# The input loaded channel-major in pieces, and one narrow projection placed on the two column halves of TensorE

## The chip, the core and the metric

The kernel runs as one program on one core of a Trainium2 chip. TensorE multiplies matrices into PSUM (8 banks of 128 partitions by 512 floats), VectorE, ScalarE and GpSimd work on SBUF and PSUM, and SyncE (SP) issues most of the transfers from and to the chip's memory. The metric is the device time of one execution in microseconds; the kernel before was executed three times, and its median is 2150.88 us. All data is float32.

## The reference

A block of 1024 tokens with 1024 channels passes two layers of computation. The first layer, to which the change belongs, begins with one wide projection of x:

```
proj = einsum("bsd,de->bse", x, w_in[l])
q, k, v, g_a, x_b, g_b, c_cols, g_c = split(proj, split_idx)
y_a = _swa_sinks(q, k, v, attn_sinks[l])        # attention over a window of 128, 8 query heads, 2 key heads
y_b = _rg_lru(x_b, ...)                         # convolution, gates, linear recurrence
y_c, v_own = _rwkv7(c_cols, rwkv_mu[l], ...)    # c_cols: r, k, v (256 each), decay input (32), rate input (32)
out = einsum("bse,ed->bsd", concat(y_a*silu(g_a), y_b*silu(g_b), y_c*silu(g_c)), w_out[l])
x = layer_norm(ALPHA * x + out)
```

`q` has 512 columns. The decay and rate inputs of the third branch are 64 columns together. Behind this stand a pooling mixer, a mixture of experts, a latent attention, a second mixture of experts and a final norm; the change does not touch their code.

## The kernel before

Every product of the first stage has channels on the contracting side, so the kernel needs x with channels on partitions: `xT`, 8 groups of 128 channels by 1024 tokens. The host hands x over token-major. `sp_first` loads it in 8 row tiles of 128 tokens by 1024 channels into `x_bufs`, with the query weights (`w_in_q`, 2 MB) behind the first four tiles. `pe_first` transposes each tile on TensorE (8 transposes of 128x128 into two PSUM banks), ScalarE copies the one bank and VectorE the other into `xT`. It handles tiles 0 to 3 (the left token half), makes four query projections for these 512 tokens, handles tiles 4 to 7, and makes the other four.

A projection (`proj`, `pe_project`) is 128 columns of weights against 512 tokens: 8 products, one for each group of channels, summed in one PSUM bank. The list `proj` gives the order: q (8), k (2), the gate of the attention (8, up to here `N_EARLY`), and then the ones that fill TensorE during the windowed attention (`pe_swa`). Banks 6 and 7 hold projections (`pj`), banks 0 to 5 the rest (`sw`). Each of the objects `pj` and `sw` hands out its banks in turn, and the user of a bank waits until the engine named in the list has emptied it.

The windowed attention runs over 8 blocks of 128 tokens with a software pipeline four deep (`turns(NT, 4)`). In turn t TensorE does the weighted sum of block t-3 (`pv`), the transposes of the probabilities of block t-2 (`tr`), the projections that `fills_at(t)` names, and the scores of block t (`sc`). Between the scores of a block and its transposes lie VectorE and ScalarE: mask, row maximum, exponential, sum, division; VectorE signals `normed` at the end. The decay/rate input (`wa`, 64 columns) is two entries of `proj`, one for each token half; both stand in turn 4. The weights of a group lie in one of two buffers (`w_view`), and SP reloads a buffer when the last projection from it is done. After turn 10 comes `prep`, which waits for everything of the attention (`after_swa`).

A product is a line

```
return e.matmul(out, lhsT, rhs, start=start, stop=stop, skip_group_check=True)      # line 221
```

so line 221 carries nearly all products of the program, and the shapes tell them apart. One float32 product appears in the trace as two MATMUL records, one transpose as one. "128\*64" in a record means that the weights have 128 rows and 64 columns. Already in the kernel before, the experts' products use the two column halves of the array when a block of 128 rows holds tokens of two experts: `pe_gate_up` and `pe_down` go over `shares(ws)`, which gives rows 0 to 63 with the one expert's weights and rows 64 to 127 with the other's, in turn:

```
for k in range(KD):
    for rows, w in shares(ws):
        m = mm(e, ring.bank[key][rows], xt[:, k, rows], gu_weights(w)[:, k, :], k == 0, k == KD - 1)
```

Of the kernel before, what the change touches and what calls it, by code (L numbers as in the profile page):

```python
# [14 lines left out]
P = 128  # L15
# [4 lines left out]
HD = 64  # L20
# [169 lines left out]
def build(nc, io):  # L190
    ctx = ExitStack()
    with ctx:
# [86 lines left out]
        base_b1 = top[0]  # L279
        x_bufs = [take(D) for _ in range(NT)]  # L280
        d_row = [landed(f"row{i}") for i in range(8)]
        d_win = [landed(f"w_in{i}") for i in range(2)]
        m_x = [d.nth() for d in d_row]
        LOADS = ["q", "kv", "ga", "rk", "vwa", "lru", "gc"]
        m_w = {name: d_win[i % 2].nth() for i, name in enumerate(LOADS)}
        w_view = {name: w_bufs[i % 2].rearrange("p a b -> p (a b)")[:, 0:KD * WIDTH[name]].rearrange("p (a b) -> p a b", a=KD)
# [35 lines left out]

        order = []
        for i in range(NT):
            order += [(("x", i, 0), "S"), (("x", i, 1), "V")]
        order += [(("v", g), "S") for g in range(2)]
# [26 lines left out]

        def x_ready(half):
            return [sw.empty(("x", 4 * half + 3, 0)), sw.empty(("x", 4 * half + 3, 1))]

        def pe_project(e, n):
            group, c0, width, half, kind, _ = proj[n]
            if n == first_of[group]:
                e.wait_ge(*m_w[group])  # L360
            if kind == "q":
                wait_all(e, x_ready(half))
            wait_all(e, pj.free(n))
            out = pj.bank[n][0:width, :]
            for k in range(KD):
                i = mm(e, out, w_view[group][:, k, c0:c0 + width], xT[:, k, half_cols(half)], k == 0, k == KD - 1)
            i.then_inc(*pj.fill(n))

        def act_project(e, n):
            group, c0, width, half, kind, j = proj[n]  # L370
            if kind == "k":
                return
            e.wait_ge(*pj.full(n))
            ps = pj.bank[n][0:width, :]
# [7 lines left out]
            out, scale = {"q": lambda: (qT[:, j, c:c + 512], HD ** -0.5), "rkv": lambda: (rkv[:, j, 1 + c:513 + c], 1.0),  # L382
                          "wa": lambda: (wa[0:64, 1 + c:513 + c], 1.0), "xb": lambda: (xb[:, j, 3 + c:515 + c], 1.0)}[kind]()
            e.activation(out, ps, ACT.Copy, bias=0.0, scale=scale).then_inc(*pj.drain(n, "S"))  # L384

# [14 lines left out]
        def pe_first(e):  # L400
            e.wait_ge(*m_const)
            for half in range(2):
                for i in range(4 * half, 4 * half + 4):
                    e.wait_ge(*m_x[i])
                    for hf in range(2):
                        key = ("x", i, hf)
                        wait_all(e, sw.free(key))
                        for k in range(4):
                            m = e.transpose(four(sw.bank[key])[:, k, :], x_bufs[i][:, P * (4 * hf + k):P * (4 * hf + k + 1)], ident)
                        m.then_inc(*sw.fill(key))  # L410
                for n in range(4 * half, 4 * half + 4):
                    pe_project(e, n)
            for n in range(8, 10):
                pe_project(e, n)
            for g in range(2):
# [7 lines left out]
                m.then_inc(*sw.fill(key))  # L423
            for n in range(10, N_EARLY):
                pe_project(e, n)

        def act_first(e):
            for half in range(2):
                for i in range(4 * half, 4 * half + 4):
                    key = ("x", i, 0)  # L430
                    e.wait_ge(*sw.full(key))
                    e.activation(xT[:, 0:4, P * i:P * (i + 1)], four(sw.bank[key]), ACT.Copy, bias=0.0).then_inc(*sw.drain(key, "S"))
# [3 lines left out]
                for n in range(4 * half, 4 * half + 4):  # L436
                    act_project(e, n)
# [4 lines left out]
            for n in range(10, N_EARLY):  # L442
                act_project(e, n)

        def dve_first(e):
            for i in range(NT):
                key = ("x", i, 1)
                e.wait_ge(*sw.full(key))
                e.tensor_copy(xT[:, 4:8, P * i:P * (i + 1)], four(sw.bank[key])).then_inc(*sw.drain(key, "V"))
                if i == 3:  # L450
                    dve_softplus(e)
            for n in range(8, N_EARLY):
                dve_project(e, n)
# [63 lines left out]
        def pe_swa(e):  # L517
            for d, n in turns(NT, 4):
# [25 lines left out]
                elif d == 0:  # L544
                    for f in fills_at(n):
                        pe_project(e, f)
                    if n == 0:
                        e.wait_ge(*pj.empty(7))
                        e.wait_ge(*pj.empty(9))
                    c0, k0, wd = window_cols(n)  # L550
# [103 lines left out]

        N_SWA = N_EARLY + 2 * NT + 4

        def sp_first(e):
            e.dma_start(chan, io["chan"]).then_inc(d_chan.sem, 16)
            for i in range(NT):
# [4 lines left out]
            e.wait_ge(*pj.full(last_of["q"]))  # L664
            e.dma_start(w_view["ga"], io["w_in_ga"]).then_inc(d_win[0].sem, 16)
# [2524 lines left out]
```

## Time and profile before

| | us |
|---|---|
| median of 3 executions | 2150.88 (2149.66 to 2151.88) |
| span of the profiled execution, first to last instruction | 2143.7 |
| TensorE busy | 2004.4 (94% of the span) |
| VectorE busy | 812.5 |
| ScalarE busy | 532.2 |
| TensorE not yet started | 5.3 |

The profile gives the span of the profiled execution and no total time for it. The three timed executions lie 6.0 to 8.2 us above that span; this is what lies around the first and the last instruction. Busy times are sums over all stages; which engine sets the end in a stage has to be read from its waits.

### The profile page before, as it was taken

The numbers are of one execution on the slowest core, as the hardware profiler recorded it, in microseconds if no ns is written. First come the engines' busy times: TensorE is split into PE (matmuls) and PEld (weight loads), VectorE is DVE, ScalarE is ACT, GpSimd is POOL, SyncE is SP. The second block draws the span as 40 slices with busy tenths as digits, with TensorE's granted clock in tenths as the row PEclk, the third lists the DMA queues.
The fourth block names the chain that finished last, engine by engine and source line by source line (L and its number), as shares of the span: only waits on it lengthen the run. The fifth ranks groups of instructions, "written<-read, shape, count | busy, mean of one in ns | idle before, by whom it ended". The sixth has DMA issues, their size and how long they took to land. (4 is left out here: it accounts for less than half of the span.)

```text
span 2143.7 us, 28374 instructions
## 1 busy us (share of the span) xinstructions
PE 2004.4 (94%) x11085; PEld 1161.1 (54%) x11085; DVE 812.5 (38%) x1889; ACT 532.2 (25%) x1294; POOL 188.4 (9%) x283
## 2 busy tenths in 40 slices
PE   8999999889997988999998999999999988999990
PEld 4545554488543964444445657777675554444440
DVE  1114555867353463111115524444352134111115
ACT  1003233433111321111133433333331110111112
POOL 0000002001162211000002000000000001000003
PEclk9999999989998989999999999999999988999995
DMA  3500100020021147999985000000020018999987
GB/s 138 226 28 6 40 20 4 1 82 4 2 90 53 41 175 302 403 423 426 424 335 204 23 0 1 1 1 1 1 80 23 30 46 331 387 425 424 425 354 265
DMA packets 51389, 334.68 MB, mean 156 GB/s; under 512 B 6832, under 2 KB 7152, under 8 KB 33200
## 3 DMA queue, kind: packets, MB, share of 16 engines
q1 hardware_dynamic: 39376, 289.63, 33.1%
q0 software_dynamic: 11872, 43.13, 5.5%
q8 instruction: 93, 1.52, 0.3%
q14 instruction: 48, 0.39, 0.1%
HBM read 285.48 MB, written 47.25 MB: 155 GB/s over the span
## 5 line engine op out<-in xcount | busy, mean ns | idle before, releaser
L221 PE MATMUL psum<-arena 128*128 128x512 f32 (+12 forms) x9694 | 1863.2, 385 | 79.6 <-issue 29.0
L221 PEld LDWEIGHTS psum<-arena 128*128 128x128 f32 (+3 forms) x9694 | 1010.5, 168 | 877.7 <-issue 783.6
L2193 DVE TENSOR_TENSOR arena<-psum,arena 128x256 f32<-128x256 f32 x50 | 21.2, 425 | 423.1 <-ACT arena L2243 423.1
L1541 ACT ACTIVATE arena<-arena 128x1024 f32<-128x1024 f32 x43 | 45.4, 1056 | 249.7 <-DVE arena L2940 105.6
L2279 POOL DMA_INDIRECT arena<-xn_rows,arena x50 | 47.2, 944 | 657.4 <-PE psum L2154 443.4
L2243 ACT ACTIVATE arena<-psum 128x256 f32<-128x256 f32 x50 | 19.2, 385 | 322.0 <-PE psum L221 322.0
L2853 ACT ACTIVATE arena<-psum,arena 128x1024 f32<-128x1024 f32 (+8 forms) x72 | 50.2, 699 | 188.6 <-DVE arena L2889 188.6
L1242 ACT ACTIVATE arena<-psum 128x256 f32<-128x256 f32 (+3 forms) x128 | 44.0, 356 | 102.3 <-PE psum L221 91.4
L2236 ACT ACTIVATE arena<-psum 128x512 f32<-128x512 f32 x50 | 29.9, 597 | 148.1 <-PE psum L221 148.1
L2882 DVE TENSOR_TENSOR psum<-psum,arena 128x128 f32<-128x128 f32 (+2 forms) x72 | 20.3, 283 | 103.5 <-PE psum L221 103.2
L2387 DVE SCALAR_TENSOR_TENSOR arena<-arena 128x1024 f32<-128x1024 f32 (+1 forms) x34 | 43.5, 1281 | 30.7 <-DMA arena<-expert_rows,arena 29.4
L2266 DVE COPY arena<-psum 128x512 f32<-128x512 f32 x50 | 34.6, 692 | 54.1 <-PE psum L221 54.1
L2154 PE MATMUL psum<-arena 128*128 128x128 f32 x400 | 51.8, 273 | 0.0
L2884 DVE TENSOR_REDUCE arena<-psum 128x1 f32<-128x1024 f32 (+8 forms) x72 | 50.8, 706 | 2.5
L2905 DVE COPY arena<-psum 128x512 f32<-128x512 f32 (+3 forms) x48 | 22.8, 489 | 76.0 <-PE psum L2808 75.9
L2224 ACT ACTIVATE arena<-psum 128x512 f32<-128x512 f32 x50 | 29.9, 597 | 87.1 <-PE psum L2154 87.1
L2393 POOL DMA_INDIRECT arena<-expert_rows,arena x34 | 34.9, 1025 | 179.3 <-issue 127.8
L2808 PE MATMUL psum<-arena 128*128 128x128 f32 x352 | 48.9, 273 | 0.0
L384 ACT ACTIVATE arena<-psum 128x512 f32<-128x512 f32 (+1 forms) x26 | 15.5, 597 | 126.1 <-PE psum L221 126.1
L2154 PEld LDWEIGHTS psum<-arena 128*128 128x128 f32 x400 | 45.4, 141 | 2.1 <-issue 2.1
L398 DVE TENSOR_TENSOR arena<-psum,arena 128x512 f32<-128x512 f32 x16 | 10.9, 689 | 87.8 <-ACT arena L379 87.7
L2940 DVE TENSOR_TENSOR arena<-arena,psum 128x512 f32<-128x512 f32 x16 | 11.0, 688 | 84.3 <-PE psum L221 84.3
(303 smaller groups left out, 1306.5 us busy)
## 6 DMA issues: line engine op xcount, KB each, us to landing
arena<-in_w_exp SPq DMA_DIRECT2D x64, 2048.0 KB, 18.4
arena<-in_w_exp SPq DMA_DIRECT2D x64, 1024.0 KB, 17.7
expert_rows<-arena SPq DMA_DIRECT2D x66, 512.0 KB, 14.9
arena<-in_x SPq DMA_DIRECT2D x16, 512.0 KB, 4.6
xn_rows<-arena SPq DMA_DIRECT2D x16, 512.0 KB, 2.6
arena<-in_w_out SPq DMA_DIRECT2D x8, 512.0 KB, 8.1
arena<-in_w_o SPq DMA_DIRECT2D x1, 4096.0 KB, 12.3
out<-arena SPq DMA_DIRECT2D x8, 512.0 KB, 5.3
```

The costliest lines, as they stand in the source:

```text
L221: return e.matmul(out, lhsT, rhs, start=start, stop=stop, skip_group_check=True)
L1242: e.activation(dst, src, ACT.Copy, bias=0.0).then_inc(*ring.drain((i, name), "S"))
L1541: return e.activation(junk, h[:, s, :], ACT.Square, accum_out=sq_sum[:, s:s + 1])
L2154: m = e.transpose(four(ring.bank[key])[:, k, :], xe[:, P * (4 * hf + k):P * (4 * hf + k + 1)], ident)
L2224: e.activation(y.xt[b % 2][:, 4:8, :], four(y.ex.bank[key]), ACT.Copy, bias=0.0).then_inc(*y.ex.drain(key, "S"))
L2266: e.tensor_copy(y.y[b % 3][:, half_cols(0)], y.ex.bank[key]).then_inc(*y.ex.drain(key, "V"))
L2279: e.indirect_dma_start(out=xe, out_offset=None, in_=xn_dram[:, :], in_offset=bass.IndirectOffsetOnAxis(idx.bitcast(I32)[:, block:block + 1 ...
L2387: e.scalar_tensor_tensor(out=h[0:n, s, :], in0=c[j][0:n, :], scalar=gates[0:n, s, j:j + 1], in1=h[0:n, s, :], op0=ALU.mult, op1=ALU.add).t ...
L2393: e.indirect_dma_start(out=c[j][0:n, :], out_offset=None, in_=y_dram[:, :], in_offset=bass.IndirectOffsetOnAxis(dest.bitcast(I32)[0:n, s, ...
L2808: m = e.transpose(four(sd.bank[key])[:, j, :], pb[:, kp:kp + P], ident)
L2853: e.activation(pb[0:n, p0:p1], part_bank(key).bank[key][0:n, 0:p1 - p0], ACT.Exp, bias=mx[0:n, 0:1], scale=SCALE, accum_out=rsu[0:n, u:u + ...
L2884: e.tensor_reduce(mx[0:n, u:u + 1], bk[0:n, 0:p1 - p0], AX.X, ALU.max).then_inc(*V.up())
```

## The change

The host now also hands over x transposed (`x_t`, 128 partitions by 8 channel groups by 1024 tokens). SP loads for each of the 8 channel groups a slice of the query weights and the left token half of that group, both straight to where they are used, and then the right token half in one transfer. The transposes, the 16 copies out of PSUM and `x_bufs` are gone. The eight query projections leave the list `proj`: the four of the left half run together in four banks of `sw`, channel group by channel group as the pieces land; the four of the right half follow one after another. ScalarE copies all eight out with the query scale.

The two `wa` projections become one entry: for each channel group one product for the left token half on output partitions 0 to 63 and one for the right half on partitions 64 to 127 of the same bank. ScalarE copies the two halves out. Since `proj` is one entry shorter in its late part, turn 8 of the attention now has one fill instead of two, and from the second half of turn 4 to turn 8 each fill is the one that before stood one place later.

```diff
-        m_x = [d.nth() for d in d_row]
+        d_right = landed("x_right")
+        m_left = [[d.nth(), d.nth()][1] for d in d_row]
+        m_right = d_right.nth()
...
-        proj = [("q", P * j, P, half, "q", j) for half in range(2) for j in range(4)]
-        proj += [("kv", 0, P, half, "k", 0) for half in range(2)]
+        proj = [("kv", 0, P, half, "k", 0) for half in range(2)]
...
-        proj += [("vwa", 256, 64, half, "wa", 0) for half in range(2)]
+        proj += [("vwa", 256, 64, None, "wa", 0)]
...
         def pe_project(e, n):
...
+            if kind == "wa":
+                for k in range(KD):
+                    for hf in range(2):
+                        i = mm(e, pj.bank[n][64 * hf:64 * hf + 64, :], w_view[group][:, k, c0:c0 + 64], xT[:, k, half_cols(hf)], k == 0, k == KD - 1)
+                i.then_inc(*pj.fill(n))
+                return
...
         def act_project(e, n):
...
+            if kind == "wa":
+                for hf in range(2):
+                    e.activation(wa[0:64, 1 + 512 * hf:513 + 512 * hf], pj.bank[n][64 * hf:64 * hf + 64, :], ACT.Copy,
+                                 bias=0.0).then_inc(*(pj.drain(n, "S") if hf else S.up()))
+                return
...
         def pe_first(e):
-            e.wait_ge(*m_const)
-            for half in range(2):
-                for i in range(4 * half, 4 * half + 4):
-                    e.wait_ge(*m_x[i])
-                    for hf in range(2):
-                        key = ("x", i, hf)
-                        wait_all(e, sw.free(key))
-                        for k in range(4):
-                            m = e.transpose(four(sw.bank[key])[:, k, :], x_bufs[i][:, P * (4 * hf + k):P * (4 * hf + k + 1)], ident)
-                        m.then_inc(*sw.fill(key))
-                for n in range(4 * half, 4 * half + 4):
-                    pe_project(e, n)
+            for k in range(KD):
+                e.wait_ge(*m_left[k])
+                for j in range(4):
+                    m = mm(e, sw.bank[("q", 0, j)], w_view["q"][:, k, P * j:P * (j + 1)], xT[:, k, half_cols(0)], k == 0, k == KD - 1)
+                    if k == KD - 1:
+                        m.then_inc(*sw.fill(("q", 0, j)))
+            e.wait_ge(*m_right)
+            for j in range(4):
+                key = ("q", 1, j)
+                wait_all(e, sw.free(key))
+                for k in range(KD):
+                    m = mm(e, sw.bank[key], w_view["q"][:, k, P * j:P * (j + 1)], xT[:, k, half_cols(1)], k == 0, k == KD - 1)
+                m.then_inc(*sw.fill(key))
...
         def fills_at(t):
-            first = N_EARLY + (2 * t if t <= NT else 2 * NT + 2 + t - NT - 1)
-            return list(range(first, first + (2 if t <= NT else 1)))
+            first = N_EARLY + (2 * t if t < NT else NT + t)
+            return list(range(first, first + (2 if t < NT else 1)))
...
         def sp_first(e):
-            e.dma_start(chan, io["chan"]).then_inc(d_chan.sem, 16)
-            for i in range(NT):
-                if i == NT // 2:
-                    e.dma_start(w_view["q"], io["w_in_q"]).then_inc(d_win[0].sem, 16)
-                e.dma_start(x_bufs[i], io["x"][P * i:P * (i + 1), :]).then_inc(d_row[i].sem, 16)
+            for k in range(KD):
+                e.dma_start(w_view["q"][:, k, :], io["w_in_q"][:, k, :]).then_inc(d_row[k].sem, 16)
+                e.dma_start(xT[:, k, half_cols(0)], io["x_t"][:, k, half_cols(0)]).then_inc(d_row[k].sem, 16)
+                if k == 1:
+                    e.dma_start(chan, io["chan"]).then_inc(d_chan.sem, 16)
+            e.dma_start(xT[:, :, half_cols(1)], io["x_t"][:, :, half_cols(1)]).then_inc(d_right.sem, 16)
             e.dma_start(w_view["kv"], io["w_in_kv"]).then_inc(d_win[1].sem, 16)
...
+    arrays["x_t"] = ktile(a["x"][0].T)
```

Three places in the order of the instructions are needed below. The first is the beginning of SP's queue, before:

```order
L658 DMA arena<-in_chan 128x66
L662 DMA arena<-in_x 128x1024 x4
L661 DMA arena<-in_w_in_q 128x4096
L662 DMA arena<-in_x 128x1024 x4
L663 DMA arena<-in_w_in_kv 128x2048
L665 DMA arena<-in_w_in_ga 128x4096
```

The same place now, down to the third pair of pieces (in all there are eight pairs, then the right half, `kv` and `ga`):

```order
L658 DMA arena<-in_w_in_q 128x512
L659 DMA arena<-in_x_t 128x512
L658 DMA arena<-in_w_in_q 128x512
L659 DMA arena<-in_x_t 128x512
L661 DMA arena<-in_chan 128x66
L658 DMA arena<-in_w_in_q 128x512
L659 DMA arena<-in_x_t 128x512
```

Half a megabyte of x was the unit to wait for, and the whole query weights stood behind four of them; now the unit is a pair of quarter-megabyte pieces, and 16 pieces stand where 5 large transfers stood.

The second is the beginning of TensorE's program with its waits, before (`dma_row` is a tile of x, `dma_w_in0` the query weights):

```order
L409 MATMUL psum<-arena 128x128 [waits dma_row0,constants]
L409 MATMUL psum<-arena 128x128 x7
L409 MATMUL psum<-arena 128x128 [waits dma_row1]
...
L221 MATMUL psum<-arena 128x512 [waits swa_out_v,swa_out_s,dma_w_in0]
L221 MATMUL psum<-arena 128x512 x7
```

and now (`dma_row` is a pair of pieces):

```order
L221 MATMUL psum<-arena 128x512 [waits dma_row0]
L221 MATMUL psum<-arena 128x512 x3
L221 MATMUL psum<-arena 128x512 [waits dma_row1]
L221 MATMUL psum<-arena 128x512 x3
L221 MATMUL psum<-arena 128x512 [waits dma_row2]
```

Products stand where transposes stood, and four products lie between two waits for pieces.

The third is TensorE in turns 4 and 8 of the attention. Turn 4 before and, behind it, turn 8 with the scores of turn 7 ahead of it (`64x128` is `pv`, `L539` is `tr`, `128x256` the scores):

```order
L221 MATMUL psum<-arena 64x128 x16
L539 MATMUL psum<-arena 128x128 x16
L221 MATMUL psum<-arena 64x512 x16
L221 MATMUL psum<-arena 128x256 x8
...
L221 MATMUL psum<-arena 128x256 x8
L221 MATMUL psum<-arena 64x128 x16
L539 MATMUL psum<-arena 128x128 x16
L221 MATMUL psum<-arena 128x512 x16
L221 MATMUL psum<-arena 64x128 x16
```

and now:

```order
L221 MATMUL psum<-arena 64x128 x16
L537 MATMUL psum<-arena 128x128 x16
L221 MATMUL psum<-arena 64x512 x16
L221 MATMUL psum<-arena 128x512 x8
L221 MATMUL psum<-arena 128x256 x8
...
L221 MATMUL psum<-arena 128x256 x8
L221 MATMUL psum<-arena 64x128 x16
L537 MATMUL psum<-arena 128x128 x16
L221 MATMUL psum<-arena 128x512 x8
L221 MATMUL psum<-arena 64x128 x16
```

Turn 4 keeps its 16 narrow products and gets 8 wide ones beside them; turn 8 loses 8 of its 16 wide ones.

## Rows read from the trace of the kernel before

**Rows 1.** The page: span, busy time by engine, granted TensorE clock in 40 slices.

```profile
span 2143.7 us, 28374 instructions
PE 2004.4 (94%) x11085; PEld 1161.1 (54%) x11085; DVE 812.5 (38%) x1889; ACT 532.2 (25%) x1294; POOL 188.4 (9%) x283
PEclk9999999989998989999999999999999988999995
```

**Rows 2.** Waits of TensorE, 0 to 560 us (total us, times, longest).

```profile
PE psum L409 <- DMA arena<-in_x: 5.3, 1, 5.3
PE psum L221 <- DMA arena<-in_w_in_q: 3.1, 1, 3.1
PE psum L221 <- ACT arena L432: 0.8, 1, 0.8
```

**Rows 3.** Timeline to 188 us, TensorE and query copies (start us, us, instructions).

```profile
5.30 5.59 PE L409 MATMUL psum<-arena 128*128 128x128 f32 x32 [5.30 <-DMA arena<-in_x]
13.95 27.73 PE L221 MATMUL psum<-arena 128*128 128x512 f32 x64 [3.06 <-DMA arena<-in_w_in_q]
21.13 0.60 ACT L384 ACTIVATE arena<-psum 128x512 f32<-128x512 f32 x1 [8.99 <-PE psum L221]
27.99 0.60 ACT L384 ACTIVATE arena<-psum 128x512 f32<-128x512 f32 x1 [6.27 <-PE psum L221]
41.52 3.66 PE L409 MATMUL psum<-arena 128*128 128x128 f32 x32
46.01 141.55 PE L221 MATMUL psum<-arena 128*128 128x512 f32 x448 [0.83 <-ACT arena L432]
73.75 0.60 ACT L384 ACTIVATE arena<-psum 128x512 f32<-128x512 f32 x1 [6.27 <-PE psum L221]
```

**Rows 4.** Timeline, copies of the first transposed banks; then the granted clock meanwhile.

```profile
7.28 0.69 DVE L449 COPY arena<-psum 128x512 f32<-128x512 f32 x1 [7.28 <-PE psum L409]
8.13 0.60 ACT L432 ACTIVATE arena<-psum 128x512 f32<-128x512 f32 x1 [1.11 <-PE psum L409]
8.99 0.69 DVE L449 COPY arena<-psum 128x512 f32<-128x512 f32 x1 [1.01 <-PE psum L409]
9.62 0.60 ACT L432 ACTIVATE arena<-psum 128x512 f32<-128x512 f32 x1 [0.89 <-PE psum L409]
10.06 0.69 DVE L449 COPY arena<-psum 128x512 f32<-128x512 f32 x1 [0.38 <-PE psum L409]
...
7.00:8.00 1.00, 1.00 (x7) 1.00 (x6) 0.69 (x1) 0.03 (x1) 0.00 (x0) 1.00 1.04 422
```

**Rows 5.** Transfers of x and query weights: first, second, all; GB/s to 14 us.

```profile
DMA to landing us min/median/max: 3.9/3.9/3.9
DMA to landing us min/median/max: 4.7/4.7/4.7
L662 SPq DMA_DIRECT2D arena<-in_x x8: 421/438/489, 1.3 to 5.3; - x8
arena<-in_w_in_q SPq DMA_DIRECT2D x1, 2048.0 KB, 10.8
GB/s 0 0 0 0 0 81 98 152 129 152 328 339 410 410 421 398 421 421 421 410 410 421 421 843 152 702 94 702 328 421 609 187 655 140 655 515 234 211 433 421
```

**Rows 6.** Groups by shape: decay/rate inputs (200 to 300 us), experts' halves (860 to 1120).

```profile
L221 PE MATMUL psum<-arena 128*64 128x512 f32 x32 | 13.9, 594 | 0.0
...
L221 PE MATMUL psum<-arena 128*64 128x512 f32 x314 | 70.4, 596 | 0.6 <-issue 0.6
```

**Rows 7.** Timeline of turn 8: last chain over the probabilities, and TensorE beside it.

```profile
305.63 2.29 DVE L645 TENSOR_REDUCE arena<-arena 128x8 f32<-128x2048 f32 x1
308.23 16.42 PE L221 MATMUL psum<-arena 128*128 128x512 f32 x64
313.25 2.29 DVE L629 TENSOR_TENSOR arena<-arena 128x2048 f32<-128x2048 f32 x1
324.58 1.97 PE L539 MATMUL psum<-arena 128*128 128x128 f32 x16
324.69 0.69 DVE L614 TENSOR_TENSOR arena<-psum,arena 128x512 f32<-128x512 f32 x1 [9.14 <-PE psum L221]
336.74 0.56 SPq L935 DMA_DIRECT2D arena<-in_w2a  x1
```

**Rows 8.** Busy us of PE, PEld, DVE, ACT, POOL by stretch; then clock, DMA share, GB/s.

```profile
400.00:440.00 40.00, 31.30 (x503) 23.42 (x505) 26.34 (x45) 9.64 (x19) 0.00 (x0) 0.79 0.01 2
920.00:960.00 40.00, 40.00 (x149) 18.08 (x148) 8.54 (x16) 7.50 (x16) 3.75 (x4) 1.00 1.01 425
```

More of the change, by code:

```diff
@@ L279, in build @@
         base_b1 = top[0]
-        x_bufs = [take(D) for _ in range(NT)]
         d_row = [landed(f"row{i}") for i in range(8)]
         d_win = [landed(f"w_in{i}") for i in range(2)]
-        m_x = [d.nth() for d in d_row]
+        d_right = landed("x_right")
+        m_left = [[d.nth(), d.nth()][1] for d in d_row]
+        m_right = d_right.nth()
         LOADS = ["q", "kv", "ga", "rk", "vwa", "lru", "gc"]
-        m_w = {name: d_win[i % 2].nth() for i, name in enumerate(LOADS)}
+        m_w = {name: d_win[i % 2].nth() for i, name in enumerate(LOADS) if name != "q"}
         w_view = {name: w_bufs[i % 2].rearrange("p a b -> p (a b)")[:, 0:KD * WIDTH[name]].rearrange("p (a b) -> p a b", a=KD)
@@ L321, in build @@
         sigmoid_in = signal("gate_sigmoid")
-        order = []
-        for i in range(NT):
-            order += [(("x", i, 0), "S"), (("x", i, 1), "V")]
+        order = [(("q", half, j), "S") for half in range(2) for j in range(4)]
         order += [(("v", g), "S") for g in range(2)]
@@ L352, in window_cols @@
             return c0, P * (n - 1) + c0, 2 * P - c0
-        def x_ready(half):
-            return [sw.empty(("x", 4 * half + 3, 0)), sw.empty(("x", 4 * half + 3, 1))]
         def pe_project(e, n):
@@ L381, in act_project @@
             c = 512 * half
[L382 to L384 removed]
+            out = rkv[:, j, 1 + c:513 + c] if kind == "rkv" else xb[:, j, 3 + c:515 + c]
+            e.activation(out, ps, ACT.Copy, bias=0.0).then_inc(*pj.drain(n, "S"))
         def dve_project(e, n):
@@ L400, in pe_first @@
         def pe_first(e):
-            e.wait_ge(*m_const)
-            for half in range(2):
-                for i in range(4 * half, 4 * half + 4):
-                    e.wait_ge(*m_x[i])
-                    for hf in range(2):
-                        key = ("x", i, hf)
-                        wait_all(e, sw.free(key))
-                        for k in range(4):
-                            m = e.transpose(four(sw.bank[key])[:, k, :], x_bufs[i][:, P * (4 * hf + k):P * (4 * hf + k + 1)], ident)
-                        m.then_inc(*sw.fill(key))
-                for n in range(4 * half, 4 * half + 4):
-                    pe_project(e, n)
-            for n in range(8, 10):
+            for k in range(KD):
[11 more added lines that the diff above has]
+                m.then_inc(*sw.fill(key))
+            for n in range(2):
                 pe_project(e, n)
@@ L423, in pe_first @@
                 m.then_inc(*sw.fill(key))
-            for n in range(10, N_EARLY):
+            for n in range(2, N_EARLY):
                 pe_project(e, n)
@@ L428, in act_first @@
             for half in range(2):
[L429 to L432, printed above, removed]
                 if half == 0:
@@ L435, in act_first @@
                     e.activation(e_, ab, ACT.Exp, scale=-1.0).then_inc(*lru_s.up())
-                for n in range(4 * half, 4 * half + 4):
-                    act_project(e, n)
+                for j in range(4):
+                    key = ("q", half, j)
+                    e.wait_ge(*sw.full(key))
+                    e.activation(qT[:, j, half_cols(half)], sw.bank[key], ACT.Copy, bias=0.0, scale=HD ** -0.5).then_inc(*sw.drain(key, "S"))
             for g in range(2):
@@ L441, in act_first @@
                 e.activation(v_tok[:, 4 * g:4 * g + 4, :], four(sw.bank[key]), ACT.Copy, bias=0.0).then_inc(*sw.drain(key, "S"))
-            for n in range(10, N_EARLY):
+            for n in range(2, N_EARLY):
                 act_project(e, n)
         def dve_first(e):
[L446 to L452, printed above, removed]
+            dve_softplus(e)
+            for n in range(N_EARLY):
                 dve_project(e, n)
@@ L653, in dve_swa @@
                         dve_shift(e, *SHIFTS[n])
-        N_SWA = N_EARLY + 2 * NT + 4
+        N_SWA = N_EARLY + 2 * NT + 3
         def sp_first(e):
-            e.dma_start(chan, io["chan"]).then_inc(d_chan.sem, 16)
-            for i in range(NT):
-                if i == NT // 2:
-                    e.dma_start(w_view["q"], io["w_in_q"]).then_inc(d_win[0].sem, 16)
-                e.dma_start(x_bufs[i], io["x"][P * i:P * (i + 1), :]).then_inc(d_row[i].sem, 16)
+            for k in range(KD):
[4 more added lines that the diff above has]
+            e.dma_start(xT[:, :, half_cols(1)], io["x_t"][:, :, half_cols(1)]).then_inc(d_right.sem, 16)
             e.dma_start(w_view["kv"], io["w_in_kv"]).then_inc(d_win[1].sem, 16)
-            e.wait_ge(*pj.full(last_of["q"]))
+            e.wait_ge(*sw.full(("q", 1, 3)))
             e.dma_start(w_view["ga"], io["w_in_ga"]).then_inc(d_win[0].sem, 16)
```

7 lines of the change are left out of this document (3 added, 4 removed).

## The prediction

> **What bounds the kernel now.** I read the page first. TensorE is busy 94% of a span of 2143.7 us, and the other engines not 40% [rows 1]. A share over the whole span proves little, so I went on to TensorE's waits in the first 560 us, the part with the change. Up to the end of the query projections there are three: 5.3 us until the first tile of x has landed, 3.1 us until the query weights have landed, 0.8 us for a copy [rows 2]. The timeline gives their places [rows 3]. Transposes of the left half run from 5.30, the query projections start at 13.95, the second transposes at 41.52, the last four query projections at 46.01. From 46.01 the products of line 221 are one unbroken piece for 141 us. The query copies say what one projection of 8 products costs: 21.13 and 27.99 are 6.86 apart, so four take 27.45, and the query stage ends at 46.01 + 27.45 = 73.5. All of this stage is on the path: what TensorE gains here moves everything behind it.
>
> In the windowed attention TensorE again never pauses; VectorE waits 9.14 us for it in turn 9 [rows 7]. So a product saved there is worth its full time, as long as the chain over the probabilities stays shorter than TensorE's turn.
>
> **Removed and moved at the start.** Before, the time from 0 to 73.5 is 54.9 of query products and 18.6 of other things: 13.95 ahead of the first product, and 4.6 between 41.4 (13.95 + 27.45) and 46.01. After, only the wait for the first pair of pieces is left ahead of the products, and nothing between the halves if the right half has landed.
>
> When does the first pair land? The first tile of x, 0.5 MB behind the small `chan`, is issued at 1.3 and lands 3.9 later, at 5.2 [rows 5]. The pair is also 0.5 MB, its first piece takes the place of `chan` in the queue, and its second is issued where the first tile was. Data runs at only 81 to 152 GB/s from 1.75 to 3.5 us and then at 330 to 420 [rows 5]. I take the first product at 4.8. The bounds: 4.3 if the quarter-megabyte pieces save the whole first issue time (0.44) and some more, 6.0 if the pair runs at 150 GB/s to its end (3.5 us of data, 1.75 ahead, some 0.7 to the signal).
>
> Do the pieces feed TensorE? A pair is used up in 4 products, 3.43 us. The second tile of x lands at 1.3 + 0.44 + 4.7 = 6.4, 1.2 after the first, and the rate is 420 GB/s from 4.2 us on [rows 5]: 0.5 MB in 1.25. TensorE is slower by a factor of 2.7, so from the second pair on no wait. The right half ends the first 6.2 MB: some 18 us, needed after 34. SP needs 0.44 for an issue, 18 of them take 8 us, no bound either. Splitting the loads is hidden behind the products; without that cover it would cost what a rival below says.
>
> What is not hidden is TensorE's slow beginning. The copies of transposed banks start at 7.28, 8.13, 8.99, then 9.62, 10.06 [rows 4]: four transposes take 0.85, 0.86, then 0.63, then 0.44. TensorE has no gap there, and the granted clock in the row of 7 to 8 us says 1.00, so the durations show what that column does not: the first 3.8 us of work ran at half speed, the 1.2 of the two levels 1.2 and 2.4 GHz. Before, this cost nothing, since the products waited for the weights until 13.95. Now the products begin with it: 3.8 us at half speed lose 1.9. Bounds: 0, and 3.8 if it lasts twice as long.
>
> The Trainium skill (TensorE: Matmul & The Clock Gate, "Part 1: The HAM clock gate") says that a throttled clock is the default and activity releases it, and that the number of slow products at the start differs from run to run. The trace agrees in the first point; for the second no run here speaks yet. Taken alone, the granted clock column would give 1.9 us more gain than the skill and the copies together.
>
> Sum at the start: 4.8 + 27.45 + 1.9 + 27.45 = 61.6 instead of 73.5, a gain of **11.9**. The 16 copies into `xT` that fall away (8 on ScalarE, 8 on VectorE) were beside TensorE but for the 0.8 already counted. The eight query copies still have their banks early: the right half begins in two banks that nobody has used, and comes back to the first one 13.7 us after the left half. VectorE's small chain (softplus) now starts at once and waits for `chan`, which stands behind four pieces; its last result is needed only in the preparation behind the attention. SP's load of the gate weights waits for the last query projection as before, and the 16 zero fills and the `rk` load behind it on the queue come with it, 11.9 earlier, as do their users.
>
> **The narrow projections.** Before, two of them, 32 records of 128 rows by 64 columns against 512 tokens, take 13.9 us [rows 6], 0.434 each; half the array's columns idle. After, there are again 32 records, alternating between the column halves. The same shape in the same alternation is in the experts: 314 records in 70.4 us, 0.224 each [rows 6]. So 32 x 0.224 = 7.2, a gain of **6.7**. The lower bound is nothing, if the halves do not overlap. I take the experts' row since order and bank use are the same. The weights are now loaded twice for each channel group, but so they are there. ScalarE has two copies of 0.6 after the one filling instead of one after each; the bank is next used after a projection of 6.86, so they are hidden.
>
> The Trainium skill (TensorEngine Tiling (Array Packing), "Tile-to-Partition Mapping", "Key Properties") warns that a change of the tiling mode drains the array. By the row of the kernel before this costs nothing new: the narrow products stood between wide ones already.
>
> The saving does not appear in turn 4, which trades a narrow projection for a wide one, but in turn 8, which loses a projection of 6.86. There the chain must be shorter. VectorE ends the last `normed` at 313.25 + 2.29 = 315.5; TensorE comes to those transposes at 324.58 [rows 7], now 6.86 earlier relative to the chain: 317.7. A margin of 2.2 us, so nothing is given back. Preparation starts at 336.74 when all of the attention is done, and with TensorE earlier all its producers are: it moves as a block.
>
> **Sum.** 11.9 + 6.7 = 18.6. The profiled span of 2143.7 becomes 2125.1. The median is 7.2 above the span, and what lies around it has no reason to change: 2150.88 - 18.6 = **2132.3**.
>
> **Rivals.** (1) The halves do not overlap, or the chain in turn 8 or a wait behind it takes the 6.7 back. For it: two copies and a margin of 2.2 us only. Against it: the experts' 0.224. Time: 2150.88 - 11.9 = 2139.0.
>
> (2) The later low stretches of the clock move. From 400 to 440 us the granted clock averages 0.79 [rows 8], so 17 us stand at the lower level, and the page shows such slices in three more places [rows 1]. They follow gaps in TensorE's work, and everything arrives 18.6 earlier. A tenth more or less of some 100 us at half speed is 5 us: 2127 to 2137.
>
> (3) It comes out slower: the pieces land one after another, each with its latency. If each quarter megabyte took the 3.9 us that the first tile took, the eighth pair would land at 0.8 + 16 x 3.9 = 63.2, and the stage would end at 63.2 + 3.4 + 27.45 = 94.1, 20.6 late; less 6.7, the time is 2164.8. It decides above 6.4 us for a pair: then the last lands at 49.6 and the stage ends 6.7 late. Against it stand 1.2 us between the first two tiles of x.
>
> The Trainium skill (DMA: Bandwidth & Descriptors, "Bandwidth") speaks against this part of the change: batch transfers to 1 MiB or more, with some 2.0 us fixed plus the bytes at 436 GB/s for each. As an estimate from that page, pieces one after another would take 2.6 us each and the kernel would come to 2144. The trace shows latencies that overlap, so I don't follow it.
>
> (4) Nothing is gained: a transfer-bound stretch behind swallows it. From 920 to 960 us the DMA engines are busy 1.01 at 425 GB/s [rows 8]. But TensorE is busy 40.0 of 40 there too, and those loads are issued from buffers that come free, not at a fixed time. Time: 2150.9.
>
> **How the numbers follow.** Chances: the forecast 0.76, (1) 0.08, (2) 0.10, (3) 0.03, (4) 0.03. Around the forecast, the first product between 4.3 and 6.0, the slow beginning up to 1.9 longer, and 1 us for the median of three (the runs shown lie within 1.2) give 2130.5 to 2136.5. To hold (1) and most of (2) the range goes to 2139.5, and below to 2129.5. A measurement of this kernel tells about 0.2%, 4.3 us: faster 0.94, same 0.03, slower 0.03.
>
> **What would show it.** First product of line 221 at 4.3 to 6.0 us; products 0.86 apart, then 0.43; no wait for a transfer after the first; last query copy near 62 instead of 73.75. The narrow group: 32 records in some 7.2 us. The last transposes of probabilities without a wait for VectorE. Span near 2125. I would be wrong if TensorE waited between pairs, if the narrow group still took 13.9, or if a wait appeared behind 300 us that was not there.

## The result, and the profile after

The changed kernel took 2128.22 us (median of 4, 2126.02 to 2131.63), the kernel before beside it 2150.27 (2142.1 to 2151.88). The ratio is 0.9907, interval 0.9884 to 0.9929: faster by 20.0 us, between 15.3 and 24.9. That is under 1%, but the interval excludes no change. The changed kernel was timed twice more, on other chips, beside the kernel before: 0.9916 (0.9900 to 0.9932) and 0.9905 (0.9884 to 0.9927). The forecast was 18.6 us less, a ratio of 0.9914.

The page of the kernel after, against [rows 1]:

```profile
span 2129.9 us, 28224 instructions
PE 1991.5 (94%) x11021; PEld 1152.8 (54%) x11021; DVE 807.7 (38%) x1881; ACT 527.2 (25%) x1286; POOL 188.6 (9%) x283
PEclk9999999899998979999998999999999989999995
```

The spans differ by 13.8 only, and the times by 20. One reason is what lies around the span. The profiled execution after took 2131.63 us for 2129.9 of span, 1.7 more, not 7.2, and a later profiled execution of before took 2145.82 for 2144.1, also 1.7 more. So the first profiled execution of before took some 2145.4 us (an estimate: 2143.7 and 1.7), 5 less than the median: it was one of the quick ones.

The start. Up to 378 us TensorE waits once, in this row, and the three waits of [rows 2] are gone:

```profile
PE psum L221 <- DMA arena<-in_x_t: 4.9, 1, 4.9
```

The timeline, against [rows 3]: the first product, the first query copy, the first of the right half and the last.

```profile
4.86 7.64 PE L221 MATMUL psum<-arena 128*128 128x512 f32 x12 [4.86 <-DMA arena<-in_x_t]
...
32.28 0.60 ACT L440 ACTIVATE arena<-psum 128x512 f32<-128x512 f32 x1 [24.74 <-PE psum L221]
...
41.72 0.60 ACT L440 ACTIVATE arena<-psum 128x512 f32<-128x512 f32 x1 [6.27 <-PE psum L221]
...
62.32 0.60 ACT L440 ACTIVATE arena<-psum 128x512 f32<-128x512 f32 x1 [6.27 <-PE psum L221]
```

The last copy comes at 62.32 instead of 73.75, 11.4 earlier. TensorE's weight loads show the slow beginning, against [rows 4]:

```profile
7.59 0.34 PEld L221 LDWEIGHTS psum<-arena 128*128 128x128 f32 x1 [0.52 <-issue]
8.44 0.34 PEld L221 LDWEIGHTS psum<-arena 128*128 128x128 f32 x1 [0.52 <-issue]
9.29 0.23 PEld L221 LDWEIGHTS psum<-arena 128*128 128x128 f32 x1 [0.52 <-issue]
9.77 0.19 PEld L221 LDWEIGHTS psum<-arena 128*128 128x128 f32 x1 [0.24 <-issue]
10.20 0.19 PEld L221 LDWEIGHTS psum<-arena 128*128 128x128 f32 x1 [0.24 <-issue]
```

They stand 0.85 apart to 9.3 us and 0.43 from then on.

The narrow projection (groups by shape, 200 to 300 us), against the first row of [rows 6]:

```profile
L221 PE MATMUL psum<-arena 128*64 128x512 f32 x32 | 7.1, 595 | 0.0
```

Turn 8 and the beginning of turn 9, against [rows 7]:

```profile
297.00 9.55 PE L221 MATMUL psum<-arena 128*128 128x512 f32 x48
...
302.03 2.29 DVE L628 TENSOR_TENSOR arena<-arena 128x2048 f32<-128x2048 f32 x1
...
306.48 1.97 PE L537 MATMUL psum<-arena 128*128 128x128 f32 x16
306.59 0.69 DVE L613 TENSOR_TENSOR arena<-psum,arena 128x512 f32<-128x512 f32 x1 [2.27 <-PE psum L221]
```

The chain over the probabilities ends at 302.03 + 2.29 = 304.3 and TensorE comes at 306.48: the margin of 2.2 us is there. That is 18.1 earlier than the 324.58 of before, and up to here no wait is new. These marks of the timeline follow the lead through the program:

| mark (us) | before | after | lead |
|---|---|---|---|
| last query copy | 73.75 | 62.32 | 11.4 |
| transposes of turn 9 | 324.58 | 306.48 | 18.1 |
| first product of the recurrence | 413.03 | 393.09 | 19.9 |
| end of the span | 2143.7 | 2129.9 | 13.8 |

Up to the transposes of turn 9 the lead is what the prediction worked out, within 0.5 us. Behind it, 1.8 is won and 6.1 lost in code that the change does not touch. That is the question for the experiments: a wait caused by the change, or the scatter of two executions.

### The profile page after: what moved, and what is told of

Read it like the earlier page. It is cut to its first block and busy times, and to the rows that moved or that the text cites. A ratio compares the mean times of both kernels' runs of the same rounds, so it can differ in the third digit from the quotient of the medians.

```text
span 2129.9 us, 28224 instructions
## 1 busy us (share of the span) xinstructions
PE 1991.5 (94%) x11021; PEld 1152.8 (54%) x11021; DVE 807.7 (38%) x1881; ACT 527.2 (25%) x1286; POOL 188.6 (9%) x283
## 5 line engine op out<-in xcount | busy, mean ns | idle before, releaser
L221 PE MATMUL psum<-arena 128*128 128x512 f32 (+12 forms) x9694 | 1858.4, 386 | 84.0 <-issue 31.1
L2224 ACT ACTIVATE arena<-psum 128x512 f32<-128x512 f32 x50 | 29.9, 597 | 86.2 <-PE psum L2154 86.2
L641 DVE TENSOR_TENSOR arena<-psum,arena 128x512 f32<-128x512 f32 (+1 forms) x32 | 18.8, 651 | 62.6 <-PE psum L221 62.6
```

The lines of the kernel that those rows point to most:

```text
L2224: e.activation(y.xt[b % 2][:, 4:8, :], four(y.ex.bank[key]), ACT.Copy, bias=0.0).then_inc(*y.ex.drain(key, "S"))
```

## Experiments

**The changed kernel again**, unaltered, twice.

> The changed kernel once more, unaltered. If the two parts gave 18.1 us by the first transposes of turn 9 (324.58 to 306.48 in the two traces) and the rest is the clock's low stretches falling elsewhere, this execution repeats 4.9 us for the first product, 62.3 for the last query copy and 306.5 for turn 9 within 0.3 us, and the start of the recurrence (393.1), the routing and the end differ from the first trace by some us. If instead a wait behind the attention gives back 5 us each time, all later marks repeat within 1 us. Total expected 18 us (13 to 23) below the kernel before.

> The changed kernel again, on the chip on which the next two run. Same marks as in its other two traces to 310 us, total 17 to 20 us below the kernel before.

Medians 2131.92 and 2131.01. Transposes of turn 9 at 306.45 and 306.91, recurrence at 393.1 and 393.65, spans 2133.0 and 2131.2. The first product comes at 4.70 and 5.00 (first trace 4.86), the last query copy at 62.28 and 62.75. So everything up to the recurrence repeats within 0.6, the recurrence too, where I had expected some us of difference; the scatter comes later: from the recurrence to the end the same kernel needs 1736.8, 1739.9 and 1737.6 us.

**The kernel before again**, for its trace.

> The kernel before once more, for its trace. Theory: its profiled execution of 2143.7 us was a quick one (the five kernels measured since need 1734 to 1740 us from the start of the recurrence to the end, it needed 1730.7). This one repeats the first 350 us within 1.5 us (query copies end at 73.8 to 75.2) and needs 1733 to 1740 for the rest. Rival: the kernel before always needs 1731 there, and the change really costs 4 to 8 us behind the attention.

It needed 1734.4 for the last part, in its first trace 1730.6. Its recurrence began at 409.69 instead of 413.03, although turn 9 stood at 324.80 beside 324.58. A single kernel moves by 3 to 4 us in each of the two parts. Its timed runs span 2143.23 to 2155.1 on this chip.

**What moves them.** Between turn 9 and the recurrence I summed, for each trace, the time at the lower level of TensorE's clock: for each stretch (1 - granted clock) x 2 x its length. The windows here show one such stretch each. The columns are TensorE's busy time and records, its granted clock, the share of the DMA engines and GB/s. Before:

```profile
355.00:360.00 5.00, 5.00 (x12) 0.74 0.00 0
360.00:365.00 5.00, 5.00 (x8) 0.58 0.11 22
```

After:

```profile
340.00:345.00 5.00, 5.00 (x9) 0.66 0.08 16
```

The kernel with whole loads (below), at the same place of its program:

```profile
350.00:355.00 5.00, 5.00 (x12) 1.00 0.05 10
```

TensorE has no gap in the records just ahead of these. A second stretch, further on, has one: TensorE waits 3.3 to 3.7 us for VectorE in every trace, and the clock falls near the end of that wait in twelve of fourteen. Before, the products behind the wait and the window:

```profile
401.55 10.55 PE L221 MATMUL psum<-arena 128*128 128x512 f32 x20 [3.68 <-DVE arena L398]
...
400.00:405.00 5.00, 3.45 (x5) 0.68 0.00 0
```

Whole loads, where the clock stays up behind the same wait:

```profile
391.08 8.85 PE L221 MATMUL psum<-arena 128*128 128x512 f32 x20 [3.31 <-DVE arena L402]
...
390.00:395.00 5.00, 3.92 (x9) 1.00 0.02 3
```

Together the two stretches give these lengths from turn 9 to the recurrence:

| at the lower level | turn 9 to the recurrence | traces |
|---|---|---|
| 0 | 83.4, 83.4 | whole loads, start only |
| 3.4 | 84.9 | before again |
| 6.8 to 6.9 | 86.2 to 86.7 | after (three traces), halves only, one by one, first with idle products |
| 10.2 to 10.3 | 88.1 to 88.5 | before, halves in a row, pieces of two groups, the two others with idle products |

Each us at the lower level costs 0.4 to 0.5 us. The stretch without a gap ahead of it comes in eight of the fourteen traces, 3.4 or 6.8 us long; the one at the wait in all but whole loads and start only, 3.4 or 6.8 us long too. The code between the two marks is the same in all, and the kernel before stands in two of the lines: the 1.8 us won here are its first trace's 10.2 against 6.8. From the recurrence to the end (less the last 45 us) the low time is some 99 to 116 us. The length less half of it is 1680.9 and 1682.6 in the two traces of before, 1683.8, 1681.9 and 1682.5 in the three of the changed kernel, and 1680.9 to 1686.5 in all fourteen, where the uncorrected lengths are 1730.6 to 1740.3. So of the 6.1 us that seemed lost, 3.2 are low clock. The other 2.9 are more than the 1.7 and 1.9 by which one kernel's traces differ from each other, but the means of the two kernels, 1681.8 and 1682.7, are only 1.0 apart. TensorE's waits behind the recurrence have the same releasers in both; the largest differences between the first traces are 2.1 us of "issue" (29.0 and 27.9 in the traces of before, 31.1 in the first after) and 1.2 for L1394 (2.9 and 4.1, in the second trace of before 3.6). No wait of the change is found there; a cost of about 1 us is not excluded. Why an execution falls to the lower level at one place and not at another is open.

**The start alone.** The decay/rate inputs are two projections again.

```diff
-        proj += [("vwa", 256, 64, None, "wa", 0)]
+        proj += [("vwa", 256, 64, half, "wa", 0) for half in range(2)]
```

> Only the start is changed; the decay/rate inputs are two projections as before. Theory: gain at the start 11.4 us, turn 9 transposes at 313.1, total 11.4 us under the kernel before (6 to 16). Rival, that the transposes cost nothing because they lay beside loading: under 4 us.

Ratio 0.9944 (0.9929 to 0.9959), 12.0 us less. First product at 4.88, last query copy at 62.63, turn 9 at 313.45. The theory holds; by the rival the gain would have been under 4 us.

**The halves alone.** The kernel before with the new `wa` entry.

> Only the decay/rate projections are changed; x is loaded and transposed as before. Theory: query copies end at 73.75 as before, the 32 narrow records take 7.1 us, turn 9 transposes come 6.7 earlier at 317.9, total 6.7 under the kernel before (2 to 11). Rival, that the saving is lost behind the attention: turn 9 at 317.9 but the start of the recurrence at 413 as before.

Ratio 0.9966 (0.9954 to 0.9979), 7.3 us less (4.5 to 9.9); the medians, 2144.31 to 2148.24, are only 3.9 apart, since its runs lie in two groups, 2138 to 2139 and 2144 to 2145. The narrow group takes 7.1 us. The recurrence began at 405.81, 3.9 and 7.2 earlier than in the two traces of before, so the saving is not lost behind the attention, as the rival had it. Turn 9 came at 319.32, not 317.9: the query copies ended at 75.16 instead of 73.75. The timeline shows where:

```profile
13.90 29.20 PE L221 MATMUL psum<-arena 128*128 128x512 f32 x64 [2.64 <-DMA arena<-in_w_in_q]
```

The four left projections took 29.20 instead of the 27.73 of [rows 3]. In this execution the clock had fallen in the wait for the weights (granted 0.93 from 10 to 14 us, 0.76 from 14 to 20). So the old start could also lose 1.4 us in that gap. The two parts alone sum to 19.3, together they gave 18.0 on this chip: they add up within the intervals.

**The halves one after the other** instead of in turn.

```diff
-                for k in range(KD):
-                    for hf in range(2):
+                for hf in range(2):
+                    for k in range(KD):
```

> The changed kernel, but the 8 products of the left column half come first and then the 8 of the right, instead of in turn. Theory (two products overlap only when they are neighbours on different halves): the 32 records take 13.5 us, 6.4 more than in turn; turn 9 at 312.9; total 6.4 above the changed kernel. Rival (TensorE finds the other half's products further back in its queue): about 7 us as before, no loss.

Ratio 0.9939 (0.9924 to 0.9953), 4.9 us worse than the changed kernel's 0.9916. The group of the narrow records, 200 to 300 us:

```profile
L221 PE MATMUL psum<-arena 128*64 128x512 f32 x32 | 12.3, 595 | 0.0
```

12.3, nearly the 13.9 of before: products overlap when they stand near each other on different halves. The theory is right in the main, its 13.5 too high, and the weight loads at the border between the two halves show why:

```profile
221.67 0.14 PEld L221 LDWEIGHTS psum<-arena 128*64 128x64 f32 x1 [0.29 <-issue]
222.10 0.19 PEld L221 LDWEIGHTS psum<-arena 128*64 128x64 f32 x3 [0.29 <-issue]
222.53 0.19 PEld L221 LDWEIGHTS psum<-arena 128*64 128x64 f32 x2 [0.24 <-issue]
222.96 0.19 PEld L221 LDWEIGHTS psum<-arena 128*64 128x64 f32 x2 [0.23 <-issue]
223.45 0.14 PEld L221 LDWEIGHTS psum<-arena 128*64 128x64 f32 x1 [0.29 <-issue]
```

Elsewhere one load comes every 0.43 us; here eight come between 222.10 and 223.45. The last four records of the left half run beside the first four of the right, which saves four times 0.43, 1.7 us. So the overlap reaches a little beyond direct neighbours, in this trace over two products on either side, and the rival has that much right. Turn 9 came at 312.57, 6.1 later than in the changed kernel: 5.2 from this group and 0.9 because the slow beginning lasted to 11.0 us here.

**Whole loads, and pieces of two channel groups.** The first edit puts the 2 MB of query weights and the 2 MB of the left half of x in one transfer each; the second doubles each piece. Both were executed once, as was the next one.

> The changed kernel with the query weights as one transfer of 2 MB and the left half of x as another, products from the time both are in. Theory: 4 MB at 420 GB/s behind 1.75 us of setting up and 0.7 to the signal: first product at 12.4 us, 7.5 later than with pieces, and everything to turn 9 as much later (314). Rival (small pieces slow the transfers down, so that whole ones land much earlier): first product under 10.

> The changed kernel with pieces of two channel groups (0.5 MB each, pairs of 1 MB). Theory: the first pair lands when 1 MB is in, 1.25 us later than half a megabyte: first product at 6.1 us, no further wait for a transfer, last query copy 1.2 later at 63.5. Rival (the fixed part of a transfer decides, not its bytes): first product within 0.3 of 4.9.

First product with whole loads:

```profile
15.34 74.89 PE L221 MATMUL psum<-arena 128*128 128x512 f32 x189 [15.34 <-DMA arena<-in_x_t]
```

First product with pieces of two groups:

```profile
6.68 83.56 PE L221 MATMUL psum<-arena 128*128 128x512 f32 x274 [6.68 <-DMA arena<-in_x_t]
```

Whole loads start 10.5 us later than the pieces, 3 more than I expected, and their last query copy comes at 73.30, where the kernel before has 73.75. So without the pieces the start gains 0.4 instead of 11.4 us. That is the balance of three terms: the second transposes and their wait, 4.6 between the halves, are still saved; the first product comes 1.4 later than the 13.95 of before; and the slow beginning, 2.8 here (weight loads 0.85 apart from 15.34 to 20.6), now falls on products. What pieces would be worth with the transposes kept, no run shows. The 4 MB needed 13.6 us from 1.75 on, 310 GB/s, where I had counted with 420. Part of that is not a slower rate: in this stretch 362 GB/s were moved, and the surplus belongs to the loads that stand behind these two in the queue. Pieces of two groups start 1.8 later, last copy at 63.82, 1.5 later. Single executions: 2137.98 and 2134.38.

**The pieces one by one**, the rival on the slower side.

```diff
+                e.wait_ge(d_row[k].sem, 16)
                 e.dma_start(xT[:, k, half_cols(0)], io["x_t"][:, k, half_cols(0)]).then_inc(d_row[k].sem, 16)
+                e.wait_ge(d_row[k].sem, 32)
```

> The changed kernel, but SP waits for each of the 16 pieces to land before it issues the next. This is the slower rival of the prediction made real. Theory: each piece alone takes some 3.0 us, a pair 6.0, TensorE waits 2.6 us ahead of each pair, the eighth pair lands near 49, last query copy near 80 and turn 9 some 18 us later than with pieces in flight together; the granted clock or the durations may fall as well. If latencies did not matter (rate alone): pair 1.3 us, no wait, nothing lost.

TensorE's timeline at the third, fourth and seventh pair and at the right half:

```profile
18.00 3.70 PE L221 MATMUL psum<-arena 128*128 128x512 f32 x8 [2.47 <-DMA arena<-in_x_t]
23.51 3.70 PE L221 MATMUL psum<-arena 128*128 128x512 f32 x8 [1.82 <-DMA arena<-in_x_t]
...
40.06 5.40 PE L221 MATMUL psum<-arena 128*128 128x512 f32 x8 [1.87 <-DMA arena<-in_x_t]
...
54.95 35.43 PE L221 MATMUL psum<-arena 128*128 128x512 f32 x75 [5.62 <-DMA arena<-in_x_t]
```

A piece alone takes 2.7 to 2.8 us from issue to landing, a pair 5.5. The last query copy comes at 85.70, 12 us later than in the kernel before and 6 later than expected: the right half is issued only at 45.6 and TensorE waits 5.62 for it, and the clock falls where the gaps are (the 8 records from 40.06 take 5.40 instead of 3.70; granted 0.92 from 24 to 45 us, 0.51 from 54 to 61). The execution took 2158.14, where the kernel before has a median of 2148.32 on this chip. In the changed kernel the pieces of a pair land 3.2 and 3.6 us after their issues, 0.45 apart: the latencies overlap, and that is what the change lives on.

**Idle products ahead of the first pair.** Two products of 512 columns on a tile of ones, whose result nobody reads (`WARM` is 2, `ones_in` waits for the tile).

```diff
         def pe_first(e):
+            e.wait_ge(*ones_in)
+            for _ in range(WARM):
+                mm(e, four(banks[7]), ones, bc_mid(ones, 4), True, True)
             for k in range(KD):
```

> The changed kernel with two idle products of 512 columns on a tile of ones ahead of the first pair, 1.2 to 4.7 us. They compute nothing that is used. Theory (the first 4 us of TensorE's work run at half speed, whichever work it is): the first real product still starts at 4.9, the slow stretch ends by 5.5, last query copy at 60.5 instead of 62.3, 1.9 less in total. Rival (full speed begins at a time, near 9.3 us, not after so much work, as both traces so far have it): last query copy at 62.3 as before.

> Two idle products on ones ahead of the first pair, as before, now beside the changed kernel on one chip. Its trace gave 60.1 us for the last query copy against 62.3. Theory: 2.2 us less in total (0 to 4). Rival: the later low stretches of the clock spread more than that, no difference to tell.

The weight loads in the first trace, the last idle one and the first three real ones:

```profile
3.09 0.34 PEld L221 LDWEIGHTS psum<-arena 128*128 128x128 f32 x1 [0.52 <-issue]
4.86 0.30 PEld L221 LDWEIGHTS psum<-arena 128*128 128x128 f32 x2 [1.44 <-DMA arena<-in_x_t]
5.40 0.19 PEld L221 LDWEIGHTS psum<-arena 128*128 128x128 f32 x1 [0.24 <-issue]
5.83 0.19 PEld L221 LDWEIGHTS psum<-arena 128*128 128x128 f32 x1 [0.24 <-issue]
```

The first real product is still at 4.86 and already at full speed; last query copy 60.10, 2.2 earlier than in the changed kernel. In the second trace the first product, at 4.92, still runs at half speed and the others do not; last query copy 60.48. So full speed does not always begin near 9.3, as the rival had it. Against a fixed time stand the whole loads too, whose products begin at 15.34 and are slow to 20.6. But the next run shows that the idle products do not always help. In total nothing shows: the first run took 2129.48 (0.9917, 0.9899 to 0.9936) without the changed kernel beside it, the second 2129.47 (0.9899, 0.9879 to 0.9919) beside 2131.01 (0.9905, 0.9884 to 0.9927) on one chip.

**The same with the pieces of x issued by ScalarE.**

> As warm2, and the left pieces of x are issued by ScalarE beside SP's weight pieces, so that a pair is issued in 0.4 us instead of 0.9. Theory: the first pair lands near 4.4 instead of 4.8; the idle products end at 4.65, so the first real product starts then, 0.2 earlier; last query copy 59.9. Rival (two queues share the same engines and slow each other): first product as before or later, and waits between the first pairs.

The first real product in the timeline, and TensorE's weight loads from there on:

```profile
5.56 84.69 PE L221 MATMUL psum<-arena 128*128 128x512 f32 x285 [0.56 <-DMA arena<-in_x_t]
...
5.56 0.50 PEld L221 LDWEIGHTS psum<-arena 128*128 128x128 f32 x2 [2.14 <-DMA arena<-in_x_t]
6.58 0.34 PEld L221 LDWEIGHTS psum<-arena 128*128 128x128 f32 x1 [0.52 <-issue]
...
9.14 0.23 PEld L221 LDWEIGHTS psum<-arena 128*128 128x128 f32 x1 [0.52 <-issue]
9.61 0.19 PEld L221 LDWEIGHTS psum<-arena 128*128 128x128 f32 x1 [0.24 <-issue]
```

The rival was right in its first half: the first piece of x is issued 0.45 earlier and lands 4.7 us after its issue instead of 3.6, so the first product comes 0.7 later. Waits between the first pairs do not appear. The last query copy comes at 62.60, 2.5 later than in the first trace with idle products. 0.7 of that is the later first product; the other 1.8 is the slow beginning, which is back: the loads stand 0.85 apart up to 9.14, although TensorE had worked from 1.22 to 5.00 on the idle products. So the theory of the idle products (the first 4 us of work are slow, whichever work it is) holds in two traces and fails in this one. Between the idle and the real products TensorE waits 0.56 us here, and the records of the other two traces show no such wait; whether that decides, no run shows. In total 2130.15 (0.9914, 0.9890 to 0.9938), no difference from the changed kernel's 2131.01.

## Why the prediction was right, and where it was off

*The gain at the start, 11.9: measured 11.4.* The first product at 4.8 was 4.86. The slow beginning was put at 1.9 and cost 2.3: 62.32 less 0.3 for the copy's delay, less 4.86 and twice 27.45. In six other traces of this start without idle products (all but the pieces one by one) it cost 1.9 to 3.1, the most in "halves in a row", where it lasted to 11.0 us. That no pair after the first is waited for was right, though the rate was not: "TensorE is slower by a factor of 2.7" counted with 420 GB/s; with the 310 GB/s of the whole loads (the changed kernel moved 343 from 1.75 to 15.34 us), half a megabyte takes 1.7 us and the factor is 2.0. The whole loads show that 11.0 of these 11.4 us need the pieces. Pieces one by one come out slower than before, as rival (3) said, at 2.7 to 2.8 us per piece instead of its 3.9. Its limit of 6.4 us for a pair was too high: pairs took 5.5 and the stage still ended 12 late, since the sum left out that the right half is issued only behind the eighth pair (5.6 us of wait) and that the clock falls meanwhile (a stretch from 54 to 61 us, some 3.4 us lost).

*The narrow projections, 6.7: measured 13.9 to 7.1 in the group and 18.1 - 11.4 = 6.7 in the marks.* The experts' row was the right price. Half of rival (1), halves that don't overlap, is nearly what "one after the other" shows; the other half, a chain in turn 8 that is longer than the turn, is excluded by the margin of 2.2.

*The preparation "moves as a block".* It did but for the clock: less half the low time, turn 9 to the recurrence takes 82.8 to 83.4 us in all fourteen traces.

*Rival (2)* turned out to be no alternative to the forecast but a scatter that lies over every execution of both kernels. This is the step that was mis-sized: "1 us for the median of three (the runs shown lie within 1.2)". The runs of the kernel before spread over 2141.47 to 2155.1, and medians of the changed kernel lay at 2128.2, 2131.9 and 2131.0. The first is 1.3 below the low end of my range. The rival's "they follow gaps in TensorE's work" is right for one of the two stretches ahead of the recurrence and wrong for the other. The mistake about the scatter is also in "the median is 7.2 above the span": 1.7 lies around a span, the other 5.5 was a quick execution. Since both enter before and after alike, the difference of 18.6 stands inside all three intervals.

The Trainium skill (DMA: Bandwidth & Descriptors, "Bandwidth") wants transfers of 1 MiB or more. Whole loads did move a little more in the stretch from 1.75 to 15.34 us, 362 GB/s against 343 with pieces. As a rule for this place the traces decide against it: whole loads lost 10.5 us at the first product. The 2.6 us for a piece alone is an estimate from the fit that the Trainium skill (DMA: Bandwidth & Descriptors, "Anatomy of one DMA — SWDGE (gpsimd) path") gives for transfers on GpSimd's path; here SyncE issues them, and the run one by one measured 2.7 to 2.8.

The Trainium skill (TensorE: Matmul & The Clock Gate, "Part 1: The HAM clock gate") says that activity releases the throttled default, and that the slow beginning varies from run to run. The 1.9 to 3.1 us agree with the second. For the first speak two of the three traces with idle products; in the third, 3.8 us of idle products ahead did not bring full speed before 9.1 us.

## What to carry to other kernels

When an engine waits for a load at the start, ask how little of it allows the first useful product, and order the pieces so that each one feeds more work than it takes to land; here 11.0 of the 11.4 us at the start needed it, and leaving out the transposes with whole loads gave 0.4. A projection that uses half the columns of the array can have its two token halves side by side, but their products must stand in turn: one half behind the other kept only 1.6 of the 6.8 us. Compare marks along the timeline before explaining a difference of totals: here the marks of the changed kernel up to the recurrence agree within 0.6 us, where its totals scatter by 10.

## What the hardware showed unexpectedly

The granted clock in the windows says 1.00 from 5 to 9 us, while TensorE works at half speed there (0.85 us between weight loads instead of 0.43). The durations, not that column, show the slow beginning. The trace's own record of the clock has its first entry where full speed begins (9.4 us after, 9.2 before, 11.1 with the halves in a row, 20.9 with whole loads); ahead of it the column reads 1.00 without an entry.

Two issuing engines made the first landing later, not earlier (4.7 us from issue instead of 3.6, one trace).

Two idle products ahead of the real ones ended the slow beginning early in two traces (the loads 0.43 apart from 4.9 and 5.8 us on) and not in a third (9.1 us).

Products on the two column halves overlapped over a short distance in the program, not only as direct neighbours: four records of 0.43 us each ran beside four of the other half.

TensorE's low stretches between turn 9 and the recurrence came as 0, 3.4, 6.8 or 10.2 us in equal code, and cost 0.4 to 0.5 of their length. One of them had no gap in the records ahead of it.
